# One inference step of a hybrid decoder: retention and memory attention of the prompt placed between the steps of the sample's latent attention

## The chip, the core and the metric

The kernel runs on one core of a Trainium2 chip, in float32. It is written for the engines directly: each engine has its own list of instructions, which it works off in order, and semaphores are waited for and counted up. TensorE (PE) multiplies matrices and writes to PSUM, VectorE (DVE) and ScalarE (ACT) do elementwise work, GpSimd (POOL) does elementwise work in SBUF and issues the gathers, and SyncE (SP) issues the other DMAs. The metric is the device time of one execution in microseconds.

## What is computed

One layer for a prompt of 2048 tokens and for a sample of 8 sequences with one new token each and 16384 tokens in a paged cache. The two parts that matter here are these, cut from the reference:

```python
def retention(q, k, v, state0):            # prompt: 16 chunks of 128 tokens, 4 heads of 128
    def step(S, inp):
        qb, kb, vb = inp
        sc = jnp.einsum('bihd,bjhd->bhij', qb, kb) * intra[None]
        o = (jnp.einsum('bhij,bjhe->bihe', sc, vb)
             + jnp.einsum('bihd,bhde->bihe', qb * q_dec[None, :, :, None], S))
        S = S * s_dec[None, :, None, None] + jnp.einsum('bjhd,bjhe->bhde', kb * k_dec[None, :, :, None], vb)
        return S, o
def mem_attend(q, mk, mv):                 # prompt: 256 memory tokens
    s = jnp.einsum('bthd,bmhd->bhtm', q, mk).astype(jnp.float32) * MEM_SCALE
    p = jax.nn.softmax(s, axis=-1).astype(mv.dtype)
    return jnp.einsum('bhtm,bmhd->bthd', p, mv).reshape(B, T, MEM_W)
def mla_sample(q_lat, q_pe, ckv_new, kpe_new, pool_ckv, pool_kpe, page_table):
    ckv_past = pool_ckv[page_table].reshape(DB, -1, KV_LORA)      # 8 x 16384 x 256
    kpe_past = pool_kpe[page_table].reshape(DB, -1, MLA_ROPE)     # 8 x 16384 x 64
    s_past = jnp.einsum('bqhc,bkc->bhqk', q_lat, ckv_past) + jnp.einsum('bqhr,bkr->bhqk', q_pe, kpe_past)
...
```

The output of retention is normalised per head (`head_norm`) and multiplied with a gain; it is joined with the others in `merge`.

## The kernel before

The kernel is a row of stages. Each stage is a function that allocates its own SBUF, PSUM and semaphores, and ends with a barrier of all engines: keys and values of the memory, the input projection, the sample's preparation, `sample_attention`, `prompt_retention_memory`, `prompt_latent_attention`, `merge`. The next stage loads its constants after the barrier.

**sample_attention** (names `sa_`) works through the cache in 64 steps of 2048 tokens. GpSimd gathers the latents (`nat`, 16 KB a partition, L1577) and the rope part (`kp`, 4 KB a partition, L1579) of step g into buffer g % DEEP, with DEEP = 4; from step 4 on it first waits until the values of step g-4 are done. In step g, VectorE turns the two halves of `nat` and then `kp` (L1612, the functions `turn(g, 0..2)`). After the first of them comes the row maximum of step g-1 (`new_low`, L1618, L1619), after the second the accumulation of step g-2 (`add_up`, L1627, L1630). TensorE multiplies the first turned piece with the queries (`scores(g, 0)`, L1709), turns the probabilities of g-1 (`pull_probs`, L1722), does `scores(g, 1)`, then the values of g-1 (`values`, L1733), which read `nat` and free its buffer, then `scores(g, 2)`. ScalarE does the exponential and one copy (L1672, L1673, L1681). PSUM holds two banks each of scores, turned probabilities and outputs.

**prompt_retention_memory** (names `rm_`) works through 16 blocks of 128 tokens, in loops of two. GpSimd rotates queries and keys (`rotate`: four products L620, L622, their sum `qk` L631, the decayed keys `kd` L636). TensorE turns queries and keys (L786, L790), multiplies queries with memory keys (L796), makes the state's increment (L804), the masked scores (L810), the outputs (L818, L819), turns the probabilities (L826), multiplies with memory values (L768) and turns the normalised output (L776). VectorE decays the queries (L660), takes the memory maximum (L664, L665), masks the scores (L668), inverts and applies the sum (L671, L673), updates the state (L679) and does the head's statistics, root, normalisation and gain (L683 to L700). Seven banks or pairs of banks of PSUM are used.

## Time and profile before

| | us |
|---|---|
| Median of three runs | 2814.61 |
| The three runs | 2814.0 to 2818.64 |
| The profiled execution's own time | 2821.66 |
| Its span | 2820.0 |
| Stage of the sample's latent attention, from its first DMA to that of the next stage | 1080.62 to 1582.75 |
| Stage of retention and memory attention, likewise | 1582.75 to 1838.61 |
| TensorE / VectorE / ScalarE / GpSimd busy in the span | 2339.9 / 1295.5 / 534.5 / 286.3 |

Times in the profile are counted from the span's start. A share of busy time over the whole span is a mean over stages with quite different limits, so the stages are to be read one by one.

### The profile page before, as it was taken

What the parts mean: (1) busy time and instruction counts of PE and PEld (TensorE: products, weight loads), DVE (VectorE), ACT (ScalarE), POOL (GpSimd) and SP (SyncE); (2) the same over time, 40 slices, a digit from 0 to 9 for tenths busy, and PEclk for the clock granted to TensorE, in tenths of its full rate; (3) what the DMA queues carried; (4) which work ended last, traced back from release to release, by engine and by line L of the source; (5) the groups of instructions that cost most, each with busy time, mean ns of one, the idle gap of its engine ahead of it and who ended that gap; (6) DMA issues with size and microseconds to landing.
All of it is one profiled execution on the core that took longest, in us unless ns stands there. A gap on an engine that the chain in (4) does not pass through costs nothing. (4 is left out here: it accounts for less than half of the span.)

```text
span 2820.0 us, 49617 instructions
## 1 busy us (share of the span) xinstructions
PE 2339.9 (83%) x20723; PEld 1925.0 (68%) x20723; DVE 1295.5 (46%) x2890; ACT 534.5 (19%) x1094; POOL 286.3 (10%) x244
## 2 busy tenths in 40 slices
PE   4499999999999685777777577748889999969998
PEld 2399999978888464555555366636766777757886
DVE  1711111110101243999888388836555444335554
ACT  1410010010100000111111133313333333332110
POOL 0000000000000001222222266500000000000000
PEclk8599999999999756999999799969999999989999
DMA  4221121111211515999999233221100000045542
GB/s 174 100 82 66 57 72 64 56 69 60 75 45 45 200 42 197 379 368 372 371 351 369 83 121 121 88 87 37 31 19 25 19 19 7 5 145 166 174 149 69
DMA packets 128029, 351.00 MB, mean 124 GB/s; under 512 B 13400, under 2 KB 74832, under 8 KB 117624
## 3 DMA queue, kind: packets, MB, share of 16 engines
q1 hardware_dynamic: 105088, 163.37, 17.0%
q0 software_dynamic: 22784, 185.35, 17.0%
q8 instruction: 121, 1.98, 0.3%
q14 instruction: 36, 0.29, 0.0%
HBM read 285.22 MB, written 63.46 MB: 124 GB/s over the span
## 5 line engine op out<-in xcount | busy, mean ns | idle before, releaser
L454 DVE COPY pj_stage<-pj_ps 128x280 f32<-128x280 f32 (+1 forms) x96 | 50.9, 530 | 642.0 <-PE pj_ps L473 334.8
L473 PE MATMUL pj_ps<-pj_wh,pj_xh 128*128 128x280 f32 x1024 | 299.1, 292 | 6.4 <-DVE pj_wl L447 6.4
L1612 DVE STREAM_TRANSPOSE sa_turned<-sa_nat 128x2048 f32<-128x2048 f32 x128 | 293.2, 2291 | 19.9 <-DMA sa_kp<-cache_kpe,sa_index 19.8
L473 PE MATMUL pj_ps<-pj_wl,pj_xh 128*128 128x280 f32 x1024 | 298.8, 292 | 0.0
L473 PE MATMUL pj_ps<-pj_wh,pj_xl 128*128 128x280 f32 x1024 | 298.8, 292 | 0.0
L1709 PE MATMUL sa_ps_s<-sa_turned,sa_q 128*32 128x128 f32 x5120 | 200.6, 288 | 100.8 <-DVE sa_turned L1612 69.8
L1709 PEld LDWEIGHTS sa_ps_s<-sa_turned,sa_q 128*32 128x32 f32 x5120 | 154.8, 115 | 134.4 <-DVE sa_turned L1612 76.0
L476 PE MATMUL pj_ps<-pj_xh,pj_wl 128*128 128x512 f32 x512 | 202.6, 396 | 0.0
L476 PE MATMUL pj_ps<-pj_xl,pj_wh 128*128 128x512 f32 x512 | 201.9, 394 | 0.0
L476 PE MATMUL pj_ps<-pj_xh,pj_wh 128*128 128x512 f32 x512 | 201.6, 394 | 0.0
L1031 DVE CUSTOM_DVE_ANT_0 la_row<-la_ps_s,la_causal 128x512 f32<-128x512 f32 (+3 forms) x160 | 97.6, 611 | 226.0 <-PE la_ps_s L1172 224.3
L473 PEld LDWEIGHTS pj_ps<-pj_wh,pj_xh 128*128 128x128 f32 x1024 | 193.4, 189 | 6.7 <-issue 6.5
L473 PEld LDWEIGHTS pj_ps<-pj_wl,pj_xh 128*128 128x128 f32 x1024 | 193.5, 189 | 0.0
L473 PEld LDWEIGHTS pj_ps<-pj_wh,pj_xl 128*128 128x128 f32 x1024 | 193.0, 188 | 0.0
L1196 PE MATMUL la_ps_o<-la_probsT,la_value 128*128 128x128 f32 x1088 | 145.6, 281 | 48.9 <-ACT la_probsT L1105 48.9
L1196 PEld LDWEIGHTS la_ps_o<-la_probsT,la_value 128*128 128x128 f32 x1088 | 132.6, 193 | 60.6 <-ACT la_probsT L1105 37.6
L436 ACT COPY pj_stage<-pj_ps 128x280 f32<-128x280 f32 (+1 forms) x96 | 44.0, 458 | 623.1 <-PE pj_ps L473 333.7
L1461 PE MATMUL mg_ps<-mg_wh,mg_ch 128*128 128x512 f32 (+1 forms) x408 | 129.0, 398 | 20.6 <-DVE mg_wl L1391 16.8
L1733 PE MATMUL sa_ps_o<-sa_nat,sa_p_turned 128*16 128x256 f32 x2048 | 133.0, 389 | 6.0 <-issue 5.5
L1461 PE MATMUL mg_ps<-mg_wl,mg_ch 128*128 128x512 f32 (+1 forms) x408 | 127.7, 395 | 0.0
L1461 PE MATMUL mg_ps<-mg_wh,mg_cl 128*128 128x512 f32 (+1 forms) x408 | 127.5, 394 | 0.0
L1577 POOL DMA_INDIRECT sa_nat<-cache_ckv,sa_index x64 | 60.0, 937 | 641.5 <-DVE sa_index L1601 332.4
(337 smaller groups left out, 4106.1 us busy)
## 6 DMA issues: line engine op xcount, KB each, us to landing
s_zn<-pj_stage SPq DMA_DIRECT2D x32, 560.0 KB, 3.0
s_zt<-pj_stage SPq DMA_DIRECT2D x16, 1024.0 KB, 3.8
rm_z<-s_zn SPq DMA_DIRECT2D x16, 768.0 KB, 4.3
mg_cat<-s_cat SPq DMA_DIRECT2D x16, 768.0 KB, 6.3
mg_gate<-s_zt SPq DMA_DIRECT2D x16, 768.0 KB, 8.0
pj_raw<-w_in POOLq DMA_DIRECT2D x8, 1120.0 KB, 6.7
pn_x<-x_prompt SPq DMA_DIRECT2D x4, 2048.0 KB, 9.1
pj_raw<-w_in POOLq DMA_DIRECT2D x8, 1024.0 KB, 5.9
```

Source lines behind the costliest of these rows:

```text
L436: act.copy(stage_view(u, w, natural), ps[:, u % QUAD, 0:(w if natural else 512)]).then_inc(ev_act, 1)
L454: dve.tensor_copy(stage_view(u, w, natural), ps[:, u % QUAD, 0:(w if natural else 512)])\
L473: mm = pe.matmul(ps[:, u % QUAD, 0:w], x[:, k, u * P:(u + 1) * P], wt[:, j, k, 0:w], **flags)
L476: mm = pe.matmul(ps[:, u % QUAD, :], wt[:, j, k, m * P:(m + 1) * P], x[:, k, c * 512:(c + 1) * 512], **flags)
L1031: dve.tensor_tensor_reduce(out=row[:, s, c * P:(c + w) * P], in0=ps_s[:, (first_chunk[u] + n) % 3, 0:w * P], in1=m, scale=1.0, scalar=-3.0 ...
L1196: mm = pe.matmul(ps_o[:, h, :], value[:, c + x, h * HD:(h + 1) * HD], probsT[:, g % 3, x, :], start=(c + x == 0), stop=(c + x == b))
L1461: mm = pe.matmul(ps[0:w, j, n * 512:(n + 1) * 512], a[:, c, :], wt[:, c, n * 512:(n + 1) * 512], start=(c == 0 and a is hi and wt is wh), ...
L1577: pool.indirect_dma_start(out=nat[:, g % DEEP, :, :].rearrange("p t c -> p (t c)"), out_offset=None, in_=ckv_rows, in_offset=where).then_i ...
L1612: dve.transpose(turned[:, s, a:z, :, :].rearrange("p c x q -> p x c q"), of.rearrange("p x (c q) -> p x c q", q=QR)).then_inc(t_ok, 1)
L1709: mm = pe.matmul(ps_s[j * QR:(j + 1) * QR, s, 0:TQ * QR], q32[:, u, c, :], turned[:, s, c, j * TQ:(j + 1) * TQ, :].rearrange("p x q -> p ( ...
L1733: mm = pe.matmul(ps_o[j * QR:j * QR + ROWS_Q, s, 0:KVL], p_turned[:, s, x, j, :], nat[:, g % DEEP, TQ * j + x, :], start=(x == 0), stop=(x ...
```

## The change

The two stages become one, `sample_attention_and_retention`. The work of block b is cut into parts that stand at fixed places of the steps 4b to 4b+4, written out without loops; the helper `begun(g, k)` gives the block whose k-th step g is. So that all fits, buffers are cut: DEEP is 3 in place of 4, `ps_p` and `ps_o` of latent attention have one bank each in place of two, and retention works with three shared PSUM areas (`bank_a`, `bank_b`, `bank_m`) and single `qk`, `kd`, `cat_r`, `cat_m`. The scaling of the memory probabilities, the normalisation of retention's output and its gain go from VectorE to ScalarE; the gain is applied to the turned output. The constants of both parts are loaded at the start, and VectorE, ScalarE, TensorE and GpSimd wait for those of retention before their first step.

```diff
-DEEP = 4
+DEEP = 3
+STRIDE = STEPS // BLOCKS
-        ps_p = r.ps("ps_p", [P, 2, 512])
-        ps_o = r.ps("ps_o", [P, 2, 512])
+        ps_p = r.ps("ps_p", [P, 512])
+        ps_o = r.ps("ps_o", [P, 512])
+        def begun(g, after):
+
+            b, rest = divmod(g - after, STRIDE)
+            return b if rest == 0 and 0 <= b < BLOCKS else None
...
+                pool.wait_ge(m_consts, 16 * M_CONSTS)
                 pool.wait_ge(index_ok, 1)
                 for g in range(STEPS):
                     if g >= DEEP:
...
+                    if begun(g, 1) is not None:
+                        rotate(begun(g, 1))
...
                     if 1 <= g <= STEPS:
                         new_low(g - 1)
+                    if begun(g, 1) is not None:
+                        decay_queries(begun(g, 1))
+                    if begun(g, 2) is not None:
+                        mask_scores(begun(g, 2))
+                        invert_total(begun(g, 2))
+                    if begun(g, 3) is not None:
+                        new_state(begun(g, 3))
+                        head_statistics(begun(g, 3))
                     if g < STEPS:
                         turn(g, 1)
                     if g >= 2:
                         add_up(g - 2)
+                    if begun(g, 1) is not None:
+                        memory_top(begun(g, 1))
...
+                def turn_queries_keys(b):
+                    pe.wait_ge(rotated, b + 1)
+                    if b >= 1:
+                        pe.wait_ge(cat_m_ok, b)
+                        pe.wait_ge(cat_r_ok, b)
...
-                for g in range(STEPS + 1):
+                pe.wait_ge(m_consts, 16 * M_CONSTS)
+                for g in range(STEPS + 2):
                     if g < STEPS:
                         scores(g, 0)
-                    if g >= 1:
+                    if 1 <= g <= STEPS:
                         pull_probs(g - 1)
                     if g < STEPS:
                         scores(g, 1)
-                    if g >= 1:
+                    if begun(g, 0) is not None:
+                        turn_queries_keys(begun(g, 0))
+                    if begun(g, 1) is not None:
+                        add_to_state(begun(g, 1))
+                    if begun(g, 2) is not None:
+                        retention_values(begun(g, 2))
+                    if begun(g, 3) is not None:
+                        turn_memory(begun(g, 3), 1)
+                    if 1 <= g <= STEPS:
                         values(g - 1)
                     if g < STEPS:
                         scores(g, 2)
+                    if begun(g, 0) is not None:
+                        memory_scores(begun(g, 0))
+                    if begun(g, 1) is not None:
+                        retention_scores(begun(g, 1))
+                    if begun(g, 2) is not None:
+                        turn_memory(begun(g, 2), 0)
+                    if begun(g, 3) is not None:
+                        memory_values(begun(g, 3))
+                        turn_retention(begun(g, 3))
```

On GpSimd, the gathers of the changed kernel are L1362 and L1364. Before, there are only pairs of gathers in a row. Now the rotation of block b follows the gather of step 4b+1:

```order
L1362 DMA sa_nat<-cache_ckv,sa_index 128x4096
L1364 DMA sa_kp<-cache_kpe,sa_index 128x1024
L1337 TENSOR_TENSOR rm_prod_cos<-rm_z,rm_rot 128x8x64
L1339 TENSOR_TENSOR rm_prod_sin<-rm_z,rm_rot 128x8x64
L1337 TENSOR_TENSOR rm_prod_cos<-rm_z,rm_rot 128x8x64
L1339 TENSOR_TENSOR rm_prod_sin<-rm_z,rm_rot 128x8x64
L1346 TENSOR_TENSOR rm_qk<-rm_prod_cos,rm_prod_sin 128x1024
L1352 TENSOR_TENSOR rm_kd<-rm_qk,rm_k_decay 128x512
```

Six operations have come between the gather of step 4b+1 and that of 4b+2.

On TensorE, a step of latent attention in the middle of its stage, from `scores(g, 0)` to `scores(g, 2)`, before:

```order
L1709 MATMUL sa_ps_s<-sa_turned,sa_q 32x128 x16
L1722 MATMUL sa_ps_p<-sa_pull,sa_probs 32x64 x16
L1709 MATMUL sa_ps_s<-sa_turned,sa_q 32x128 x16
L1733 MATMUL sa_ps_o<-sa_nat,sa_p_turned 16x256 x16
L1709 MATMUL sa_ps_s<-sa_turned,sa_q 32x128 x8
```

and now, for a step g = 4b:

```order
L1622 MATMUL sa_ps_s<-sa_turned,sa_q 32x128 x16
L1635 MATMUL sa_ps_p<-sa_pull,sa_probs 32x64 x16
L1622 MATMUL sa_ps_s<-sa_turned,sa_q 32x128 x16
L1656 MATMUL rm_bank_a<-sa_ident,rm_qk 128x128 x4
L1659 MATMUL rm_bank_b<-sa_ident,rm_qk 128x128 x4
L1646 MATMUL sa_ps_o<-sa_nat,sa_p_turned 16x256 x16
L1622 MATMUL sa_ps_s<-sa_turned,sa_q 32x128 x8
L1668 MATMUL rm_bank_m<-rm_mkT,rm_mq 128x256 x4
```

The transposes of the rotated queries and keys stand in front of the values of step g-1, the memory scores behind the step's last scores.

On VectorE, a step of latent attention before:

```order
L1612 STREAM_TRANSPOSE sa_turned<-sa_nat 128x16x4x32
L1618 TENSOR_REDUCE sa_step_top<-sa_ps_s 128x1
L1619 SCALAR_TENSOR_TENSOR sa_low<-sa_step_top,sa_low 128x1
L1612 STREAM_TRANSPOSE sa_turned<-sa_nat 128x16x4x32
L1627 SCALAR_TENSOR_TENSOR sa_acc<-sa_acc,sa_ratio,sa_total 128x1
L1630 SCALAR_TENSOR_TENSOR sa_acc<-sa_acc,sa_ratio,sa_ps_o 128x256
L1612 STREAM_TRANSPOSE sa_turned<-sa_kp 128x16x2x32
```

and now, for a step g = 4b+3 (the row of "..." leaves out the root's eleven small operations):

```order
L1399 STREAM_TRANSPOSE sa_turned<-sa_nat 128x16x4x32
L1405 TENSOR_REDUCE sa_step_top<-sa_ps_s 128x1
L1406 SCALAR_TENSOR_TENSOR sa_low<-sa_step_top,sa_low 128x1
L1447 SCALAR_TENSOR_TENSOR rm_state<-rm_state,rm_bank_b 128x128 x4
L1452 BN_STATS rm_stats<-rm_bank_m 128x6 x4
L1455 BN_AGGR rm_mean_var<-rm_stats 128x2 x4
L1457 TENSOR_SCALAR rm_var<-rm_mean_var 128x4
...
L1461 SCALAR_TENSOR_TENSOR rm_shift<-rm_mean_var,rm_root 128x4
L1399 STREAM_TRANSPOSE sa_turned<-sa_nat 128x16x4x32
L1414 SCALAR_TENSOR_TENSOR sa_acc<-sa_acc,sa_ratio,sa_total 128x1
L1417 SCALAR_TENSOR_TENSOR sa_acc<-sa_acc,sa_ratio,sa_ps_o 128x256
```

State, statistics and root of block b stand between the first and the second transpose of that step.

## Rows read from the trace of the kernel before

**Rows 1.** Busy time by stage, latent attention of the sample, then retention and memory.

```profile
core 0: us, PE busy (x) PEld busy (x) DVE busy (x) ACT busy (x) POOL busy (x), PEclk, DMA share, GB/s
1080.62:1582.75 502.13, 348.92 (x9243) 260.59 (x9243) 421.37 (x471) 65.11 (x257) 119.96 (x128) 0.92 0.86 339
1582.75:1838.61 255.86, 173.13 (x1216) 156.28 (x1216) 191.56 (x561) 72.77 (x192) 151.70 (x96) 0.91 0.35 115
```

**Rows 2.** Timeline, one clean step: start, duration, engine, line, operation, count, idle before.

```profile
1154.25 2.27 DVE L1612 STREAM_TRANSPOSE sa_turned<-sa_nat 128x2048 f32<-128x2048 f32 x1
...
1156.45 0.25 DVE L1618 TENSOR_REDUCE sa_step_top<-sa_ps_s 128x1 f32<-128x128 f32 x1
...
1156.81 2.30 DVE L1612 STREAM_TRANSPOSE sa_turned<-sa_nat 128x2048 f32<-128x2048 f32 x1
...
1159.17 1.08 PE L1709 MATMUL sa_ps_s<-sa_turned,sa_q 128*32 128x128 f32 x32 [0.81 <-DVE sa_turned L1612]
...
1160.06 1.91 PE L1733 MATMUL sa_ps_o<-sa_nat,sa_p_turned 128*16 128x256 f32 x32
1160.68 2.27 DVE L1612 STREAM_TRANSPOSE sa_turned<-sa_nat 128x2048 f32<-128x2048 f32 x1
...
1161.79 0.62 PE L1709 MATMUL sa_ps_s<-sa_turned,sa_q 128*32 128x128 f32 x16
1162.28 0.94 POOL L1577 DMA_INDIRECT sa_nat<-cache_ckv,sa_index  x1 [4.26 <-PE sa_ps_o L1733]
...
1163.52 0.94 POOL L1579 DMA_INDIRECT sa_kp<-cache_kpe,sa_index  x1 [0.30 <-issue]
```

**Rows 3.** Rope gather's landing, its transposes, start of the stage, TensorE's waits.

```profile
DMA to landing us min/median/max: 9.3/10.5/16.5
...
L1612 DVE STREAM_TRANSPOSE sa_turned<-sa_kp x64: 1201/1236/1241, 1109.5 to 1560.7; 128x1024 f32<-128x1024 f32 x64
...
1095.21 1.01 POOL L1577 DMA_INDIRECT sa_nat<-cache_ckv,sa_index  x1 [332.37 <-DVE sa_index L1601]
...
1105.06 4.50 DVE L1612 STREAM_TRANSPOSE sa_turned<-sa_nat 128x2048 f32<-128x2048 f32 x2 [10.13 <-DMA sa_kp<-cache_kpe,sa_index]
...
PE sa_ps_s L1709 <- issue: 30.9, 22, 3.2
```

**Rows 4.** Timeline of a late block of retention, VectorE and TensorE.

```profile
1820.79 1.22 DVE L664 TENSOR_REDUCE rm_top<-rm_ps_m 128x4 f32<-128x1024 f32 x1
...
1822.12 0.69 DVE L668 TENSOR_TENSOR rm_scT<-rm_ps_sc,rm_mask 128x512 f32<-128x512 f32 x1
...
1822.87 0.49 PE L818 MATMUL rm_ps_a<-rm_z,rm_scT 128*128 128x128 f32 x2 [0.35 <-DVE rm_scT L668]
...
1824.20 0.18 DVE L671 RECIPROCAL rm_inv<-rm_total 128x4 f32<-128x4 f32 x1 [1.39 <-ACT rm_probs L720]
...
1824.53 0.39 PE L819 MATMUL rm_ps_a<-rm_state,rm_qT 128*128 128x128 f32 x2
...
1825.56 0.88 DVE L679 SCALAR_TENSOR_TENSOR rm_state<-rm_state,rm_ps_st 128x128 f32<-128x128 f32 x4
1825.70 1.09 PE L826 MATMUL rm_ps_m<-rm_ident,rm_probs_n 128*128 128x128 f32 x8 [0.78 <-DVE rm_probs_n L673]
...
1830.18 1.37 DVE L695 TENSOR_SCALAR rm_normed<-rm_ps_a,rm_mean_var,rm_root 128x128 f32<-128x128 f32 x4
```

**Rows 5.** Timeline of the first rotation on GpSimd: first product and sum.

```profile
1595.08 1.25 POOL L620 TENSOR_TENSOR rm_prod_cos<-rm_z,rm_rot 128x512 f32<-128x512 f32 x1 [50.98 <-DMA rm_mq<-s_zt]
...
1600.28 2.34 POOL L631 TENSOR_TENSOR rm_qk<-rm_prod_cos,rm_prod_sin 128x1024 f32<-128x1024 f32 x1 [0.16 <-POOL rm_prod_sin L622]
```

**Rows 6.** A constant's landing (us last), a small operation's mean, the stage's last accumulation.

```profile
rm_gain<-ret_gn_g SPq DMA_DIRECT2D x1, 256.0 KB, 5.9
...
L665 DVE TENSOR_SCALAR rm_bias<-rm_top 128x4 f32<-128x4 f32 x16 | 12.5, 780 | 0.6
...
1569.63 0.48 DVE L1630 SCALAR_TENSOR_TENSOR sa_acc<-sa_acc,sa_ratio,sa_ps_o 128x256 f32<-128x256 f32 x1 [4.51 <-PE sa_ps_o L1733]
```

More of the change, by code:

```diff
@@ new lines, in invert_total, with new_state @@
+                def invert_total(b):
+                    dve.wait_ge(exp_ok_m, b + 1)
+                    if b >= 1:
+                        dve.wait_ge(pn_ok, b)
+                    dve.reciprocal(m_inv[:, :], m_total[:, :]).then_inc(inv_ok, 1)
+                def new_state(b):
+                    dve.wait_ge(out_ps, b + 1)
+                    dve.wait_ge(st_ps, b + 1)
+                    for h in range(HEADS):
+                        last = dve.scalar_tensor_tensor(state[:, h, :], state[:, h, :], S_DEC[h], bank_b[:, h, :], ALU.mult, ALU.add)
+                    last.then_inc(state_ok, 1)
@@ new lines, in head_statistics @@
+                def head_statistics(b):
+                    for h in range(HEADS):
+                        last = dve.bn_stats(stats[:, h, :], bank_c[:, h, :])
+                    link(last)
+                    for h in range(HEADS):
+                        last = dve.bn_aggr(mean_var[:, h, :], stats[:, h, :])
+                    link(last)
+                    link(dve.tensor_scalar(var[:, :], mean_var[:, :, 1], EPS, None, ALU.add))
+                    if b >= 1:
+                        dve.wait_ge(normed_ok, b)
+                    inverse_root(dve, link, var[:, :], root[:, :], tmp[:, :])
+                    dve.scalar_tensor_tensor(shift[:, :], mean_var[:, :, 0], -1.0, root[:, :], ALU.mult, ALU.mult)\
+                       .then_inc(root_ok, 1)
@@ new lines, in memory_out, with normalise @@
+                def memory_out(b):
+                    act.wait_ge(pv_ps_m, b + 1)
+                    if b >= 1:
+                        act.wait_ge(cat_m_out, 16 * b)
+                    act.copy(cat_m[:, :, :], bank_a[:, :, :]).then_inc(cat_m_ok, 1)
+                def normalise(b):
+                    act.wait_ge(root_ok, b + 1)
+                    if b >= 1:
+                        act.wait_ge(rT_ps, b)
+                    for h in range(HEADS):
+                        last = act.activation(normed[:, h, :], bank_c[:, h, :], ACT.Identity, bias=shift[:, h:h + 1],
+                                              scale=root[:, h:h + 1])
+                    last.then_inc(normed_ok, 1)
@@ new lines, in turn_memory @@
+                def turn_memory(b, n):
+                    pe.wait_ge(pn_ok, b + 1)
+                    if n == 1:
+                        pe.wait_ge(pT_ok, 2 * b + 1)
+                    halves = bank_m[:, 2:4, :].rearrange("p h (m q) -> p h m q", m=2)
+                    for h in range(2):
+                        for x in range(2):
+                            mm = pe.transpose(halves[:, h, x, :], m_probs[:, 2 * n + h, x * P:(x + 1) * P], ident[:, :])
+                    mm.then_inc(pT_ps, 1)
@@ new lines, in memory_values, with turn_retention @@
+                def memory_values(b):
+                    pe.wait_ge(pT_ok, 2 * b + 2)
+                    for h in range(HEADS):
+                        for n in range(2):
+                            mm = pe.matmul(bank_a[:, h, :], mv[:, n, h * HD:(h + 1) * HD], probsT[:, h, n, :],
+                                           start=(n == 0), stop=(n == 1))
+                    mm.then_inc(pv_ps_m, 1)
+                def turn_retention(b):
+                    pe.wait_ge(normed_ok, b + 1)
+                    pe.wait_ge(state_ok, b + 1)
+                    for h in range(HEADS):
+                        mm = pe.transpose(bank_b[:, h, :], normed[:, h, :], ident[:, :])
+                    mm.then_inc(rT_ps, 1)
@@ L1738, in _ @@
+                pe.wait_ge(m_consts, 16 * M_CONSTS)
+                for g in range(STEPS + 2):
                     if g < STEPS:
                         scores(g, 0)
-                    if g >= 1:
+                    if 1 <= g <= STEPS:
                         pull_probs(g - 1)
```

539 lines of the change are left out of this document (227 added, 312 removed).

## The prediction

> **What bounds the kernel now.** I read the busy table by stage first [rows 1]. The sample's latent attention takes 502.1 us and retention with memory attention 255.9 us; the change touches these 758 us and nothing else. In the first VectorE is busy 421 of 502 us and the DMA engines 0.86 of the time, in the second TensorE 173 and VectorE 192 of 256 us, with DMA at 0.35. So the first stage has little room on two resources, and the second has latencies to hide.
>
> Then the timeline of one clean step [rows 2]. Times in a step are counted from the start S of its first transpose. The three transposes, the row maximum and the two accumulations fill VectorE: the next step begins 6.43 us later (1154.25 to 1160.68). On the average a step takes 7.16 us, since the 64 transposes of keys' rope part start between 1109.5 and 1560.7 [rows 3]: 0.7 us a step goes to disturbances, among them fetches of instructions on TensorE (30.9 us before the score matmuls alone [rows 3]). TensorE ends the values of the step before at S + 7.72 (1161.97), and GpSimd issues the next gather at once, at 1162.28. It was waiting: with four buffers the gather g waits for the values of g-4. The rope half follows 1.24 us later (1163.52).
>
> How long does a gather need? The rope half lands at least 9.3 us after its own issue [rows 3], so both halves have landed at least 10.54 us after the first issue; with an empty queue at the start of the stage it was 9.85 us (1095.21 to 1105.06 [rows 3]). I take 10.54, the steady value. With four buffers a gather has two steps of 6.43 us and the rest of the third to arrive, 19.3 - 8.0 = 11.3 us: just enough.
>
> **The change: three buffers.** The gather g+2 is now issued after the values of g-1, which end in step g. It must be there two steps after S. So two steps cost at least 7.72 + 0.31 + 10.54 = 18.6 us, 9.3 us a step instead of 6.43, before anything is added. That is the heart of my forecast: the stage passes from a bound of work to a loop of latencies, and what is put between a step's start and the end of its values lengthens that loop.
>
> **The change: what is added between.** Four kinds of step follow each other; A is the one before a multiple of four, then B, C, D. On VectorE, ahead of the second transpose: in C 0.69 us (decayed queries, the same form as the mask), in D 0.69 + 0.18 (mask, reciprocal), in A the state, the statistics and the root, 4.62 us from 1825.56 to 1830.18 and one small operation of 0.2, 4.82 in all. After it, in C, the memory maximum, 1.22 and a small operation like the reciprocal, 0.2 [rows 4]. Together 7.8 us a block; the scaled probabilities, the normalisation and the gain go to ScalarE. On TensorE, ahead of the values: in B eight transposes, 1.09 us; in C four matmuls, half of the eight's 2.05 us (1822.87 to 1824.92), so 1.03; in D these eight, 2.05; in A four transposes, 0.55 [rows 4]. ScalarE's parts (at most 4 x 0.5 us in a step) lie beside TensorE's and VectorE's work; they cost nothing while that cover of 2 us is there. Loads and stores of retention, 1.66 MB a block, find a queue that idles more than a third of the time. On SP they are queued in the order of the blocks, more than a block ahead of need, so nothing.
>
> On GpSimd the rotation stands behind every fourth gather: four products and the sum take 7.54 us (1595.08 to 1602.62 [rows 5]), then the decayed keys. TensorE meets the wait for the rotation in B, in front of the values of A.
>
> **The loop, one block (four steps).** From the end of the values in A: 0.31 to GpSimd, 2.5 for the two issues, 7.54 of rotation, 1.09 of transposes, 1.91 of values [rows 2]: 13.35. Gather of D: 0.31 + 10.54 = 10.85. Step D to the end of the values in it: 2.56 to the end of the maximum and the new minimum, 0.87, 2.36 for the second transpose, 0.89 of scores, 2.05, 1.91: 10.64. Then TensorE ends the scores 0.44 later (1162.41), and A, whose first transpose is over by then, goes on: maximum and minimum 0.36 (1156.45 to 1156.81), 4.82, 2.36, 0.89, 0.55, 1.91: 11.33. Sum **46.2 us**. A second loop, gathers of C and A without the rotation, is 10.85 + (2.56 + 0.69 + 2.36 + 0.89 + 1.03 + 1.91 = 9.44) + 10.85 + (2.56 + 4.82 + 2.36 + 0.89 + 0.55 + 1.91 = 13.09) = 44.2. The first is the longer. To it comes a part of the disturbances. Before they cost 4 x 0.73 = 2.9 us in four steps; the queue is now less full and half of them fall beside waits, so between 0 and 3, and I take 1.0: 47.2 us a block.
>
> **Start and end.** GpSimd now waits for seven more constants ahead of its first gather; like-sized ones land 5.9 us after issue [rows 6], so the first gather starts about 6 us late, at 1101.3, and step 0 at 1111.2. Step 3 ends its values at 6.5 + 9.44 + 10.85 + 13.09 = 39.9 us after that, 1151.1. Fifteen blocks of 47.2 us lead to 1859. The last memory values, copies and value matmuls take some 8.4 us (VectorE waited 4.51 us for the last values before 1569.63 [rows 6], and some 4 us of retention stand ahead of them now), and from there the old end of the stage, 1569.63 to 1582.75, is 13.1. The next stage begins at about 1881 instead of 1838.6 [rows 1]: **+42 us**. One stage's start (10 to 15 us) is saved in this already. The profiled execution has a span of 2820.0 and 2821.66 us in all, 7 above the median of 2814.61; I add the difference to the median: **2857 us**.
>
> **A rule against the trace.** The Trainium skill, Trainium Kernel Development and Optimization, Best Practices, says that double-buffering gets DMA beside compute; by it three buffers are more than enough and the first rival below holds. The trace has GpSimd waiting for the values at four [rows 2], which speaks against it. The skill's DMA: Bandwidth & Descriptors (Anatomy of one DMA, SWDGE) gives 2.0 us plus bytes over 436 GB/s, an estimate of 8.0 us for the 2.62 MB of a step where the trace has 10.54; by it the loops are 43.7 and 39.1 us and the time is about 2820.
>
> **Rivals.** (1) The ring is not what binds; the busiest engine is. Then VectorE's 4 x 7.16 + 7.8 = 36.4 us is a block (TensorE's 348.92 / 64 x 4 + 173.13 / 16 is 33), and the time 2857 - 15 x 10.8 = 2695, **faster** by 4%. For it: the idle time of the second stage disappears and all engines have room. Against: the 11.3 us that a gather has now. It decides where 10.54 us of landing would be hidden; any loop under 44.4 us a block (47.2 - 42/15) makes the change a gain, so a landing of 7.7 us would do. 12%, and 8% for something between it and 2800. (2) The rotation is not on the path (GpSimd starts it earlier, or TensorE's wait is covered): 44.2 + 1.0 = 45.2, and 2857 - 30 = 2827. 18%, with 2800 to 2835. (3) It is worse: the new loads and stores share the DMA engines with a gather that now counts in full (landing at the median 10.5 + 1.24 = 11.7), VectorE and GpSimd disturb each other, as where an operation on 128x4 numbers took 780 ns on the mean beside the rotation [rows 6], disturbances stay at 2.9. That is 1.2 + 0.9 + 1.9 = 4 us more a block, 2917. 15%. (4) That the change does not do what it says is excluded by the order of the instructions.
>
> **Chances and range.** The forecast, 2835 to 2885: 47%. A difference under 0.2%, 5.6 us, can hardly be told from none. Slower by more than that: the forecast, rival 3 and two thirds of rival 2, some more: 68%. Within it 8%. Faster: rival 1, the case between and the rest of rival 2: 24%. The range, with rival 1 left out below and the far end of rival 3 above: 2795 to 2915.
>
> **What would show it.** In the changed profile: steps of 11 to 12 us instead of 7.2; VectorE's first transpose waiting for the rope gather in most steps, some 20 us in the whole stage before and well over 100 after; VectorE's and DMA's busy share in the stage down to 0.7 and 0.6; GpSimd's gather released by the values each time; TensorE's transposes of the rotated queries waiting some 5 us for GpSimd in each block; the stage about 800 us long. A first transpose that seldom waits for DMA makes me wrong in the direction of rival 1. A landing time much under 10 us does too. No wait of TensorE for the rotation is rival 2.

## The result, and the profile after

| | before | after |
|---|---|---|
| Median, us | 2816.62 (4 runs, 2814.0 to 2822.51) | 2929.24 (4 runs, 2928.31 to 2935.09) |
| Span of the profiled execution | 2820.0 | 2928.5 |
| The two stages, then the one | 758.0 | 859.9 |
| Mean time from one block's rotation to the next | | 51.2 |

The changed kernel takes 1.0401 times as long, with an interval of 1.0379 to 1.0424: slower by 113 us, where +42 was forecast and +100 was the end of the range. The stage takes 101.9 us more than the two did together, the stages behind it 6.6.

The row of the whole stage, and of 500 us in its middle, answers to [rows 1]. Columns: stretch, its length, busy time of PE, PEld, DVE, ACT, POOL with their instructions, TensorE's granted clock, DMA share, GB/s.

```profile
1080.62:1940.55 859.93, 596.05 (x10459) 437.04 (x10459) 595.19 (x949) 193.48 (x641) 254.43 (x224) 0.82 0.63 232
...
1200.00:1700.00 500.00, 362.26 (x6390) 266.12 (x6380) 362.76 (x550) 119.30 (x395) 157.08 (x138) 0.83 0.65 238
```

TensorE does the same 10459 matmuls as in the two stages before and is busy 596 us with them instead of 522: they became slower, not more. The granted clock fell with it: 0.82 over the whole stage, where the two stages before had 0.92 and 0.91 [rows 1]. VectorE's and DMA's shares, 0.73 and 0.65 in the middle, are about those that the prediction asked for.

Who waited for whom in the changed kernel: us in all, times, longest.

```profile
POOL sa_nat L1362 <- PE sa_ps_o L1646: 518.7, 61, 13.2
...
PE sa_ps_s L1622 <- DVE sa_turned L1399: 161.6, 57, 20.4
DVE sa_turned L1399 <- DMA sa_kp<-cache_kpe,sa_index: 159.2, 58, 17.6
...
PE rm_bank_a L1656 <- POOL rm_qk L1346: 71.5, 15, 4.8
DVE sa_step_top L1405 <- PE sa_ps_s L1622: 68.8, 40, 4.0
```

This is the loop that was forecast: each gather released by the values, VectorE waiting for the gather, TensorE waiting 4.8 us a block for the rotation.

The rotations' sums and the rope transposes, each with the start of its first and its last:

```profile
L1346 POOL TENSOR_TENSOR rm_qk<-rm_prod_cos,rm_prod_sin x16: 2339/2343/2347, 1108.8 to 1876.6; 128x1024 f32<-128x1024 f32 x16
```

```profile
L1399 DVE STREAM_TRANSPOSE sa_turned<-sa_kp x64: 1202/1237/1243, 1115.5 to 1915.9; 128x1024 f32<-128x1024 f32 x64
```

Fifteen blocks in 767.8 us are 51.2 us each, where 47.2 were forecast; 63 steps in 800.4 are 12.7.

One block of the changed kernel on the timeline. Columns: start, duration, engine, line, operation, count, idle before and what ended it. A to D are the steps as in the prediction, and V_A is the value matmuls (L1646) in step A, and so on: V_A starts at 1303.20, V_B at 1317.66, V_D at 1342.87, the next V_A at 1355.57. GpSimd issues the next gather 0.3 us after they end.

```profile
1300.29 1.93 PE L1622 MATMUL sa_ps_s<-sa_turned,sa_q 128*32 128x128 f32 x32 [4.12 <-DVE sa_turned L1399]
...
1303.20 2.60 PE L1646 MATMUL sa_ps_o<-sa_nat,sa_p_turned 128*16 128x256 f32 x32
...
1306.12 0.94 POOL L1362 DMA_INDIRECT sa_nat<-cache_ckv,sa_index  x1 [11.21 <-PE sa_ps_o L1646]
...
1308.32 1.30 POOL L1337 TENSOR_TENSOR rm_prod_cos<-rm_z,rm_rot 128x512 f32<-128x512 f32 x1
...
1308.95 4.35 DVE L1414 SCALAR_TENSOR_TENSOR sa_acc<-sa_acc,sa_ratio,sa_total 128x1 f32<-128x1 f32 x1
...
1313.36 2.34 POOL L1346 TENSOR_TENSOR rm_qk<-rm_prod_cos,rm_prod_sin 128x1024 f32<-128x1024 f32 x1
...
1315.76 1.11 PE L1656 MATMUL rm_bank_a<-sa_ident,rm_qk 128*128 128x128 f32 x4 [4.77 <-POOL rm_qk L1346]
...
1317.66 3.62 PE L1646 MATMUL sa_ps_o<-sa_nat,sa_p_turned 128*16 128x256 f32 x32
...
1321.58 0.97 POOL L1362 DMA_INDIRECT sa_nat<-cache_ckv,sa_index  x1 [4.75 <-PE sa_ps_o L1646]
...
1332.26 2.31 DVE L1399 STREAM_TRANSPOSE sa_turned<-sa_nat 128x2048 f32<-128x2048 f32 x1 [3.82 <-DMA sa_kp<-cache_kpe,sa_index]
...
1334.62 1.28 PE L1622 MATMUL sa_ps_s<-sa_turned,sa_q 128*32 128x128 f32 x32 [3.56 <-DVE sa_turned L1399]
...
1337.87 1.93 PE L1622 MATMUL sa_ps_s<-sa_turned,sa_q 128*32 128x128 f32 x32 [1.05 <-DVE sa_turned L1399]
...
1342.87 1.92 PE L1646 MATMUL sa_ps_o<-sa_nat,sa_p_turned 128*16 128x256 f32 x32
```

The two large terms that are not TensorE's are as forecast: D's gather lands 10.68 us after its issue (10.54 forecast), the rotation takes 7.38 (7.54). But the 32 value matmuls, which take 1.92 us in V_D at a granted clock of 1.00 (2.4 GHz), take 3.62 after the wait for the rotation, at a granted clock of 0.50 (1.2 GHz), and 2.60 in V_A, at 0.72; 32 score matmuls take 1.93 instead of 1.08, at 0.50 too.

One row stands out on VectorE: the accumulation of the sum (L1414), an operation on 128x1 numbers that takes 0.18 us elsewhere, takes 4.35 beside GpSimd's products. Here it costs nothing: VectorE then still waits 2.26 us for the next gather, and TensorE waits for the rotation until 1315.76. The experiments come back to it.

### The profile page after: what moved, and what is told of

Same layout as the page of the kernel before. It is cut to its first block and busy times, and to the rows that moved or that the text cites. A ratio compares the mean times of both kernels' runs of the same rounds, so it can differ in the third digit from the quotient of the medians.

```text
span 2928.5 us, 49100 instructions
## 1 busy us (share of the span) xinstructions
PE 2418.7 (83%) x20723; PEld 1950.2 (67%) x20723; DVE 1279.2 (44%) x2809; ACT 590.6 (20%) x1286; POOL 269.0 (9%) x244
## 5 line engine op out<-in xcount | busy, mean ns | idle before, releaser
L1622 PE MATMUL sa_ps_s<-sa_turned,sa_q 128*32 128x128 f32 x5120 | 209.3, 308 | 162.4 <-DVE sa_turned L1399 161.6
L1646 PE MATMUL sa_ps_o<-sa_nat,sa_p_turned 128*16 128x256 f32 x2048 | 155.0, 454 | 1.0 <-ACT sa_p_turned L1524 1.0
L1362 POOL DMA_INDIRECT sa_nat<-cache_ckv,sa_index x64 | 60.7, 948 | 856.6 <-PE sa_ps_o L1646 518.7
```

The lines of the kernel that those rows point to most:

```text
L1362: pool.indirect_dma_start(out=nat[:, g % DEEP, :, :].rearrange("p t c -> p (t c)"), out_offset=None, in_=ckv_rows, in_offset=where).then_i ...
L1622: mm = pe.matmul(ps_s[j * QR:(j + 1) * QR, s, 0:TQ * QR], q32[:, u, c, :], turned[:, s, c, j * TQ:(j + 1) * TQ, :].rearrange("p x q -> p ( ...
L1646: mm = pe.matmul(ps_o[j * QR:j * QR + ROWS_Q, 0:KVL], p_turned[:, s, x, j, :], nat[:, g % DEEP, TQ * j + x, :], start=(x == 0), stop=(x == ...
```

## Experiments on the loop: ring and rotation

**Three buffers alone.** The kernel before, with DEEP = 3 and nothing else.

```diff
-DEEP = 4
+DEEP = 3
```

> The kernel before with one line changed, three gather buffers in place of four; the two stages stay apart. If the ring of buffers is what binds (my forecast), two steps cost 7.72 + 0.31 + 10.54 = 18.6 us, 9.3 us a step in place of 7.16, and the whole becomes 64 x 2.14 = 137 us longer, about 2952 us, with VectorE waiting for the rope gather in nearly every step. If TensorE's clock also falls in those waits, it is more, up to 2990. If the ring does not bind and the cost of the change is the placing of retention between the steps, this stays within 20 us of the kernel before.

Measured 2984.6 us, ratio 1.059 [1.057, 1.061]. VectorE's waits for the rope gather and TensorE's for VectorE:

```profile
PE sa_ps_s L1709 <- DVE sa_turned L1612: 221.4, 45, 12.6
DVE sa_turned L1612 <- DMA sa_kp<-cache_kpe,sa_index: 198.3, 37, 9.9
```

The ring of three is a loop of latencies, as argued: 167 us on 64 steps, 2.6 us a step where the sum gave 2.1. The expectation had left room for this, up to 2990 us if the clock falls, and the granted clock is 0.80 between 1200 and 1700 us: the same symptom without anything of the retention.

**Four buffers in the changed kernel.** They fit into SBUF.

```diff
-DEEP = 3
+DEEP = 4
```

> The changed kernel with one line changed back, four gather buffers. If the ring binds in the changed kernel, a block falls from 51.3 us to what the busiest engine asks, VectorE with 36.4 us plus up to 4 us in which it is held beside the rotation, so 37 to 42 us, and the time from 2929 to between 2730 and 2790, under the kernel before. If the placing of retention is the cause, the time stays within 20 us of 2929.

Measured 2860.6 us, ratio 1.015 [1.012, 1.018]: 69 us faster than the changed kernel, but far from what was expected. VectorE waits only 18.9 us for gathers now, so the ring is gone; the block is 45.9 us. What took its place is told in the section on the hold.

**The rotation's four products left out** (constants stand in their place, so the prompt's retention isn't computed), once with three buffers and once with four.

```diff
-                    for a in range(2):
-                        pool.tensor_tensor(prod_cos[...], zz[...], cos[...], ALU.mult).then_inc(g_chain, 1)
-                        pool.tensor_tensor(prod_sin[...], zz[...], sin[...], ALU.mult).then_inc(g_chain, 1)
-                    pool.wait_ge(g_chain, 4 * (b + 1))
+                    if b == 0:
+                        pool.memset(prod_cos[...], 0.5).then_inc(g_chain, 1)
+                        pool.memset(prod_sin[...], 0.25).then_inc(g_chain, 1)
+                        pool.wait_ge(g_chain, 2)
```

> The changed kernel with its three buffers; the rotation's four products on GpSimd are left out (constants stand in their place, so the prompt retention computes something else), its sum and the decayed keys stay. Theory A (the rotation is on the loop, from the values to the next values, and TensorE's clock falls because of its waits): 5.0 us of products leave the loop of 52.4 us, TensorE's wait of 4.8 us for the rotated queries disappears, and the block is 45 to 47.5 us: 2825 to 2860 us. If the clock recovers with that wait, a block is up to 3 us less again, 2780 to 2825 us. Rival B (rotation beside the path, the gathers' loop alone sets the block): 2910 to 2930 us.

> Four buffers and the rotation's four products left out (constants in their place, so the prompt retention computes something else). Theory A: against four buffers alone the 7.1 us a block of held operations disappear, 46.4 to about 39 us: 2740 to 2760 us; the floor is VectorE's work, 36.4 us a block, 2710. Rival B (the clock of TensorE, 2.4 GHz only part of the time, and the order of its groups set the block at four buffers): 2830 to 2860 us.

Measured 2898.0 (ratio 1.0285 [1.0255, 1.0315]) and 2785.9 us (0.9894 [0.9865, 0.9923]). With three buffers 5.0 us of work a block went and TensorE's wait for the rotation with it, yet only 31 us came back, 2.1 a block. That is the distance between the two loops of the prediction (46.2 and 44.2): the second takes over at once, and it too is slower than forecast, 49.1 us against 45.2. Its gather of C lands 11.86 us after its issue on the mean, 1.3 more than the 10.54 of the sum; the granted clock is 0.85. Both expectations missed this result; the working of the prediction had it. With four buffers the same edit gives 75 us, again between the two expectations.

## Experiments on the order of TensorE's work

**Values ahead of the inserted groups**, three buffers.

```diff
+                    if 1 <= g <= STEPS:
+                        values(g - 1)
                     if begun(g, 0) is not None:
                         turn_queries_keys(begun(g, 0))
...
-                    if 1 <= g <= STEPS:
-                        values(g - 1)
```

> The changed kernel with three buffers; on TensorE the inserted part of each step stands behind the values of the step before, no longer in front of them, so that the gather is released earlier. If the ring binds, the loop loses the wait for the rotation's transposes (the gather then follows the rotation directly), 2 us of values of retention in step D and 0.5 to 1 in A: 51.3 becomes 44 to 47 us a block and the time 2820 to 2865. If TensorE's own order does not matter, 2929.

Measured 2890.0 us, ratio 1.0266 [1.0243, 1.0288]: 39 us of the 65 to 110 expected. A row of VectorE shows what ate into it (count, busy time, mean of one in ns, idle before):

```profile
L1406 DVE SCALAR_TENSOR_TENSOR sa_low<-sa_step_top,sa_low 128x1 f32<-128x1 f32 x64 | 90.2, 1410 | 2.2
```

The new minimum (L1406), 160 ns in the changed kernel, takes 5.5 us in each of 15 blocks: with the values earlier it meets GpSimd's products, 5.0 us too much a block. The section on the hold tests this in other kernels; in this one it wasn't taken away.

**TensorE kept busy.** 24 added transposes, which nothing reads, ahead of the wait for the rotated queries, 24 ahead of the second scores in A, 16 at the end of C (line of the first shown).

```diff
+                        for _ in range(24):
+                            pe.transpose(bank_a[:, 0, :], ident[:, :], ident[:, :])
                     pe.wait_ge(rotated, b + 1)
```

> The changed kernel with added transposes of the unit matrix, which nobody reads, where TensorE waits: 24 ahead of the wait for the rotation, 16 at the end of step C, 24 ahead of the second score matmuls of step A. If the 4 to 5 us a block by which my sum was too small are TensorE's lower granted clock (0.84 in place of 0.95), the clock rises over 0.92 and the time falls by 40 to 70 us, to 2860 to 2890. If the clock is not the cause, the added work is in the way and the time is 2929 or more.

Measured 2925.2 us, ratio 1.037 [1.034, 1.04]. The clock rose from 0.83 to 0.93 and the time hardly moved. It looked like the end of the theory of the clock, but the profile has a wait of TensorE that the changed kernel doesn't have:

```profile
PE sa_ps_p L1635 <- ACT sa_probs L1516: 61.4, 14, 4.4
```

In these 14 blocks the minimum (L1406) takes 4.3 to 5.5 us. What that means shows only in a kernel further down. Two kernels with fewer transposes at other places came first: 16 ahead of the first scores in C and 20 ahead of the second in A, without and with the products.

> merged_without_products (2898.0 us, 49.1 us a block from one rotated block to the next, granted clock 0.83 to 0.86), with 36 small transposes a block added on TensorE that nothing reads: 16 ahead of the first scores of the step after a block's first, 20 ahead of the second scores of the step with the head statistics. There TensorE stood for 4.25 and 4.98 us, and 24 such transposes took 4.9 us at 1.2 GHz, so they end before what it waits for. Theory A (the time above the forecast is TensorE at 1.2 GHz after its waits): what follows these waits runs at 2.4 GHz, some 4 us of the loop come back, a block of 45 to 46 us, 2840 to 2860 us. Rival B (the clock falls, but the work at 1.2 GHz lies beside the gathers): 2890 to 2905 us.

> The changed kernel with its rotation and three buffers (2929.2 us, 51.2 us a block), with the same 36 added transposes at the same two places, and none ahead of the wait for the rotated queries, where those of merged_kept_busy stood in the way. Theory A: the scores, inserted groups and values after the two waits run at 2.4 GHz, 2 to 3 us a block less, 2885 to 2900 us; what follows the wait for the rotation stays slow. Rival B: 2922 to 2935 us.

Measured 2864.5 (ratio 1.0171) and 2917.9 us (1.0355 [1.0318, 1.0391]). Without the products 34 us came back, more than rival B allows and less than A wants; with them 11, again between the two. Then all three waits of the longer loop, 30, 14 and 30 transposes, made to fit them:

> The changed kernel, with 74 added small transposes a block on TensorE that nothing reads, placed into the waits of the longer loop and made to fit them: 30 (3.6 us at 2.4 GHz) ahead of the wait for the rotated queries (4.77 us), 14 ahead of the first scores of the step with the mask (3.6 us), 30 ahead of the second scores of the step with the statistics (4.1 us). In merged_kept_busy_two_waits the block was 50.5 us, and what followed the wait for the rotation still ran at 1.2 GHz: transposes 2.0 and values 3.6 us instead of 1.1 and 1.9. Theory A (what is above the forecast is TensorE at 1.2 GHz): these run at 2.4 GHz, 2.5 us come off, and the rest of the two other steps: 47.2 to 48.5 us a block, 2865 to 2895 us, which is the forecast's block. Rival B (the second loop, or something not in the forecast, sets the block): 2905 to 2925 us.

Measured 2926.2 us, ratio 1.0409 [1.0372, 1.0446], clock 0.92: nothing gained. But its timeline tells why. A block's end there:

```profile
1292.54 0.94 POOL L1362 DMA_INDIRECT sa_nat<-cache_ckv,sa_index  x1 [9.21 <-PE sa_ps_o L1646]
...
1294.74 1.28 POOL L1337 TENSOR_TENSOR rm_prod_cos<-rm_z,rm_rot 128x512 f32<-128x512 f32 x1
1294.82 4.86 DVE L1406 SCALAR_TENSOR_TENSOR sa_low<-sa_step_top,sa_low 128x1 f32<-128x1 f32 x1
...
1300.49 1.08 PE L1635 MATMUL sa_ps_p<-sa_pull,sa_probs 128*32 128x64 f32 x32 [4.39 <-ACT sa_probs L1516]
```

The steps D and A had shrunk to 10.53 us (gather landed to the end of V_D; forecast 10.64) and 11.39 (V_D to V_A; forecast 11.33). With that the gather of B, issued after V_D at 1281.15, lands at 1292.30, just when V_A ends; its first transpose, 2.31 us, goes ahead of VectorE's minimum (L1406), and the minimum, 0.16 us of work on 128x1 numbers, now starts 0.08 us behind GpSimd's first product. It ends 4.86 us later, when the four products are done. The same happens in 13 of the 15 blocks. From here on this is called the hold: a small VectorE operation stands still beside GpSimd's work. Exponential, turned probabilities and V_B come late, and TensorE has a new wait of 4.39 us, after which it is slow again (1.08 us for 32 matmuls that take 0.65).

## Experiments on the hold

**Products behind the minimum.** The last kernel, with GpSimd waiting for the minimum first; and the same edit alone in the changed kernel.

```diff
                     if begun(g, 1) is not None:
+                        if g >= STRIDE:
+                            pool.wait_ge(low_ok, g - 1)
                         rotate(begun(g, 1))
```

> merged_kept_busy_three_waits (2926.2 us, 51.3 us a block), and GpSimd also waits for VectorE's minimum of the step before it begins a block's products. In that run three of the four steps took what was forecast (10.5 and 11.4 us for the last two), but the minimum, an operation on 128x1 numbers with both inputs in SBUF, came 0.1 us behind the start of the products and stood 4.9 us beside them instead of 0.16; TensorE waited 4.4 us for the probabilities and fell to 1.2 GHz again. Theory A (clock and hold together are the excess over the forecast): both are gone, 47 to 48.5 us a block, 2865 to 2895 us. Rival B (something else keeps the block at 51): 2915 to 2930 us.

> The changed kernel, and GpSimd waits for VectorE's minimum of the step before it begins a block's products; nothing is added on TensorE. In the changed kernel the minimum is 160 ns on the mean, before the products as it is. Theory A (there the hold is not what lengthens the loop, the clock is): no change, 2922 to 2936 us. Rival B (the hold costs here too): under 2910 us.

Measured 2854.3 us (ratio 1.0131 [1.0098, 1.0164]) and 2930.1 us (1.04 [1.0383, 1.0418]). The first is the forecast's 2857, and 11 us under its own expectation. Its stretch in the middle and one pass from V_D's gather to V_B's:

```profile
1200.00:1700.00 500.00, 429.18 (x7854) 341.81 (x7846) 366.20 (x631) 128.03 (x431) 171.87 (x152) 0.99 0.72 268
```

```profile
1276.27 0.94 POOL L1362 DMA_INDIRECT sa_nat<-cache_ckv,sa_index  x1 [10.18 <-PE sa_ps_o L1648]
...
1287.66 0.93 POOL L1362 DMA_INDIRECT sa_nat<-cache_ckv,sa_index  x1 [9.21 <-PE sa_ps_o L1648]
...
1289.87 0.16 DVE L1408 SCALAR_TENSOR_TENSOR sa_low<-sa_step_top,sa_low 128x1 f32<-128x1 f32 x1
...
1290.11 1.29 POOL L1337 TENSOR_TENSOR rm_prod_cos<-rm_z,rm_rot 128x512 f32<-128x512 f32 x1 [0.26 <-DVE sa_low L1408]
...
1291.35 1.27 POOL L1339 TENSOR_TENSOR rm_prod_sin<-rm_z,rm_rot 128x512 f32<-128x512 f32 x1
...
1292.17 0.47 DVE L1416 SCALAR_TENSOR_TENSOR sa_acc<-sa_acc,sa_ratio,sa_total 128x1 f32<-128x1 f32 x1
...
1298.60 1.92 PE L1648 MATMUL sa_ps_o<-sa_nat,sa_p_turned 128*16 128x256 f32 x32
...
1300.83 0.96 POOL L1362 DMA_INDIRECT sa_nat<-cache_ckv,sa_index  x1 [2.18 <-PE sa_ps_o L1648]
```

The clock is 0.99, and from one gather to the next V_D to V_A takes 11.39 us (forecast 11.33) and V_A to V_B 13.17 (forecast 13.35). The mean block is 46.4 us; the loop's sum was 46.2. In the changed kernel itself the wait changes nothing: there the minimum comes before the products anyway. So the four kernels with neither cure, with the transposes alone, with the wait for the minimum alone and with both take 2929.2, 2926.2, 2930.1 and 2854.3 us. It is the clock that lengthens the changed kernel's loop; the hold stands behind it and takes over as soon as the clock is cured alone. One thing moved along: the hold of the sum's accumulation (L1416 here) is shorter too, 525 ns on the mean instead of 1196. That this is worth nothing was tested only with four buffers, below.

**The hold with four buffers.** In merged_deep4 the products run one step earlier, beside the head statistics. VectorE and GpSimd there:

```profile
1327.66 1.28 POOL L1337 TENSOR_TENSOR rm_prod_cos<-rm_z,rm_rot 128x512 f32<-128x512 f32 x1
...
1328.21 4.41 DVE L1457 TENSOR_SCALAR rm_var<-rm_mean_var 128x4 f32<-128x4 f32 x1
...
1332.66 2.36 POOL L1346 TENSOR_TENSOR rm_qk<-rm_prod_cos,rm_prod_sin 128x1024 f32<-128x1024 f32 x1
1332.85 2.19 DVE L103 TENSOR_SCALAR rm_root<-rm_tmp 128x4 int32<-128x4 int32 x1
```

Moved one gather earlier, with the sum's 128x1 accumulation on VectorE as before and moved to ScalarE:

```diff
-                    if begun(g, 1) is not None:
-                        rotate(begun(g, 1))
+                    if begun(g, 0) is not None:
+                        rotate(begun(g, 0))
```

```diff
-                    dve.scalar_tensor_tensor(acc[:, u, KVL:KVL + 1], acc[:, u, KVL:KVL + 1], ratio[:, s:s + 1], total[:, s:s + 1],
-                                             ALU.mult, ALU.add)
...
+                    act.activation(acc[:, u, KVL:KVL + 1], acc[:, u, KVL:KVL + 1], ACT.Identity, bias=total[:, s:s + 1],
+                                   scale=ratio[:, s:s + 1]).then_inc(sum_ok, 1)
```

> The changed kernel with four gather buffers, and the rotation one gather earlier in GpSimd's order, so it runs in the step before the one with the head statistics. With four buffers alone the time was 2860.6 and a block 46.4 us; in it the 128x4 operations of the head statistics stood still for 7.1 us a block beside GpSimd's products. Theory A (VectorE's small operations are held by GpSimd's products): the hold leaves the statistics, and only the 128x1 accumulation of the step's sum meets the products now, held for up to 4.4 us: a block of 42 to 44 us, 2795 to 2825 us. Rival B (the 7 us are the operations' own cost there, or the loop over the score matmuls sets the block): no change, 2850 to 2865 us.

> The same as four_buffers_rotation_earlier, and the 128x1 accumulation of the sum, whose two inputs are both in SBUF, is done by ScalarE, so that it is not among VectorE's operations beside the products. Theory A: no hold is left on VectorE but the minimum of the next step, a block of 39 to 40 us, 2745 to 2775 us, faster than the kernel before. Rival B: as its partner without the moved sum, within 6 us.

Measured 2780.8 us (ratio 0.9871 [0.9843, 0.99]) and 2770.8 us (0.9833 [0.9804, 0.9862]): 80 us less than merged_deep4 with the first step alone, and both 1.3 to 1.7% faster than the kernel before. The first is faster than theory A's range. The move of the sum can't be told from nothing (the intervals overlap, the blocks are 40.1 and 40.3 us), though it took away 2.2 us of hold a block (L1414, 720 ns on the mean): in the stage VectorE waits 52.1 us for scores with the hold and 88.0 without it, so the hold had stood in the place of a wait.

Then TensorE's inserted groups behind the last scores of a step, or between values and last scores, with the rotation early:

```diff
-                    (inserted groups)
                     if 1 <= g <= STEPS:
                         values(g - 1)
                     if g < STEPS:
                         scores(g, 2)
+                    (inserted groups)
```

> four_buffers_rotation_earlier (2780.8 us, 40.1 us a block) with the inserted groups of TensorE behind the values and behind the last scores of a step, so that they are not ahead of the scores for which VectorE's maximum waits (62.6 us in all there). Theory A (VectorE is the bound now, at 0.86 busy, and its waits for the scores are what is left): 2 to 3 us a block less, 2735 to 2755 us. Rival B (the inserted work only moves from one side of the values to the other): 2772 to 2785 us.

> four_buffers_rotation_earlier with the inserted groups behind the values and ahead of the last scores. The values, and with them the next gather, are earlier by 1 us a step on the mean, the scores are not. Theory A (VectorE's waits for scores count, not the gather's start): 2772 to 2785 us, no change. Rival B (the gathers still set the time): 2735 to 2760 us.

Measured 2819.8 (ratio 1.0013) and 2859.0 us (1.0144): 39 and 78 us slower than with the order left alone, against both theories. The minimum (L1406) in the first and in the second, mean of one in ns after its busy time, 160 being its own:

```profile
L1406 DVE SCALAR_TENSOR_TENSOR sa_low<-sa_step_top,sa_low 128x1 f32<-128x1 f32 x64 | 55.4, 866 | 2.2
```

```profile
L1406 DVE SCALAR_TENSOR_TENSOR sa_low<-sa_step_top,sa_low 128x1 f32<-128x1 f32 x64 | 84.3, 1318 | 2.2
```

Earlier values mean an earlier rotation, and it meets the minimum. The last pair takes the holds away (wait for the minimum, sum on ScalarE), with the groups last and with the order left alone:

> four_buffers_earlier_groups_last (2819.8 us, 43.0 us a block; the minimum 866 and the sum's accumulation 446 ns on the mean where 160 and 179 are their own, 62 us too much in all) with both holds taken away: the products wait for the minimum, the 128x1 accumulation of the sum is on ScalarE. Theory A (the hold is why this order was slower than its partner): 39 to 40 us a block, 2755 to 2775 us. Rival B (the order itself costs): 2805 to 2825 us.

> four_buffers_rotation_earlier_sum_moved (2770.8 us, 40.3 us a block), and the products wait for the minimum, which stood at 255 ns on the mean instead of 160 there, 6 us in all. Theory A: at most these 6 us come back, 2762 to 2774 us. Rival B (the start of the rotation counts for more): 2776 us or more.

Measured 2773.4 us (ratio 0.9844 [0.9827, 0.986]) and 2770.7 us (0.9837 [0.982, 0.9854]), both theory A. The first gains 46 us over its partner with the holds (its rival B, that the order itself costs, would have left it at 2805 or more). All kernels with four buffers on one line, what stood still (busy time of VectorE's held operations over their own, in 16 blocks) beside the block:

| | held, us a block | block, us |
|---|---|---|
| rotation beside the statistics (merged_deep4) | 6.5 | 45.9 |
| the same, no products | 1.9 | 41.0 |
| rotation earlier | 2.2, on the sum | 40.1 |
| ... sum moved | 0.4 | 40.3 |
| ... groups last | 2.8 minimum, 1.1 sum | 43.0 |
| ... values first | 4.6 minimum, 0.5 sum | 45.3 |
| ... groups last, no hold | 0.1 | 40.1 |
| ... order left alone, no hold | 0.0 | 40.0 |

A hold of the statistics or of the minimum costs from half to somewhat more than its length (1.9 to 6.5 us held, 1.0 to 5.9 above the 40.0 of the last line); one of the sum's accumulation costs nothing.

## Why the prediction was wrong

**Right: what the change does.** Ring and rotation make a loop from values to values, and the kernel gets slower. DEEP = 3 alone costs 167 us. Landing, rotation, steps of 12.7 us (a little above the 11 to 12 asked for), the waits and the two shares are as listed under what would show it. Start and end are right too: the next stage starts at 1940.5 instead of the forecast 1881, 59.5 us later, and fifteen blocks of 51.2 instead of 47.2 us are 59.8. The rest of the miss, some 13 us, is the 6.6 us of the later stages and the 7 by which the profiled execution of before lay above its median, which I took off; that of after, 2930.17, lies 0.9 above its own.

**Wrong: the sum "The loop, one block".** Its terms of TensorE (values 1.91, scores 0.89, transposes 1.09 and 0.55, outputs 2.05) come from [rows 2, 4], where TensorE waits 0.81 us at most. In the loop it waits three times a block for 3.6 to 4.8 us (the three rows with such a wait above), and the granted clock falls to the lower level, 0.50, at or shortly behind each. In the block shown, from V_A's start to the next V_A's: V_A +0.69, V_B +1.71, the eight transposes +0.81 (1.90 from the first's start to the values'), the second scores in D +0.85, the outputs +1.08, the second scores in A +0.85, the memory transposes +0.50. That is 6.5 us; the block's excess is 52.4 - 46.2 = 6.2 (it is a longer one; the mean block, 51.2, is 5.0 above the sum). With the clock held up and the minimum kept clear of the products the block is 46.4 us and the time 2854.3 us: the terms themselves were right, their clock was not. The forecast knew the clock column [rows 1] and didn't use it.

**Wrong: disturbances, 1.0 us.** This was the place for it, and rival 3 had a wrong list: its 4 us were landing, VectorE beside GpSimd and the old disturbances. On the loop of the forecast none of them grew: D's gather lands after 10.69 us on the mean of 15, VectorE's hold in the changed kernel costs nothing, and TensorE's idle time that nothing in the profile ends, which the prediction took for fetches, is 9.8 us in the stage, where the score matmuls alone had 30.9. (The gather of C, which lies on the second loop only, lands after 11.78.) That rival 3 would have given 2917, near the 2929, is luck. The chances didn't add up either: the forecast, rival 3 and two thirds of rival 2 are 74%, not 68.

**Missed: the hold.** The 780 ns of [rows 6] were named, in rival 3, as a small general burden of 0.9 us. It is up to 4 or 5 us a block, and its cost depends on which operation meets the products: nothing in the changed kernel, where it is the sum's accumulation, and several us in merged_deep4 (the statistics), merged_kept_busy_three_waits and four_buffers_earlier_groups_last (the minimum), as the kernels show in which it was taken away. The minimum is held in merged_values_first, merged_kept_busy and four_buffers_earlier_values_first too, where its cost wasn't isolated. For the miss of the forecast itself it isn't needed.

**Rivals 1 and 2.** Four buffers and the rotation out of the way give 2771, a gain, but with VectorE at 0.80 to 0.86 and not at its bound of 36.4 us a block (2695). So rival 1 was right in direction once both were gone, but not in size. Rival 2, the rotation off the path, is merged_without_products: 31 us under the changed kernel where 30 was worked out.

**Open** is what fills the 40 us of the best kernels above VectorE's 36.4; their clock is 0.91 to 0.92, and VectorE still waits for scores (L1408 behind L1630, 92.3 us in the one without holds). Open, too, is what the second loop has above its sum beyond the late gather of C: without the products and with a clock of 0.93 the block is 47.4 us, not 44.2.

## What to carry to other kernels

When a change turns a stage bound by work into a loop with waits of several us, price TensorE's share of the loop at the lower clock, and look at the granted clock of a stage that already waits like that. Before cutting a ring of buffers, add the landing time and the time from landing until the buffer is free and divide by the buffers: that is the least time of a step. Here a step's values run in the next step, so a buffer is in use for a whole step and 7.7 us: with three buffers (0.3 + 10.5 + 9.3 + 7.7) / 3 = 9.3 us (9.8 measured, at a lower clock), with four less than the 6.43 of the work. One buffer was worth 167 us, more than the 120 that the merging could hide at most by rival 1. Work on GpSimd that reads and writes SBUF is to be placed by which VectorE operation it meets: a tiny one on the critical path can cost as much as a whole run of GpSimd's instructions. And when a cure moves nothing, look for a new wait before dropping the theory.

## What the runs showed of the hardware

- **The hold.** A VectorE operation of 160 to 180 ns on 128x1 or 128x4 numbers from SBUF to SBUF (the scalar_tensor_tensor with two inputs in SBUF, the tensor_scalar with one) that starts beside GpSimd's tensor_tensor ends together with one of these, mostly with the last of an unbroken row: 4.35, 4.41 and 4.86 us beside four products of 1.25 each, 2.19 beside the sum. It isn't always the last: with the products behind the minimum, the sum's accumulation ended with the second product in 9 of 15 blocks (0.47 us in the rows above) and with the fourth in 6; in the kernel before, L665 of [rows 6] ended with the first in 12 of 15 (0.73 us). In merged_values_first the minimum starts 0.5 us ahead of the first product, during the rope gather's issue, and is held all the same (5.5 us; starts on GpSimd are rough in the profile). What decides this stays open. Transposes of 128x2048 (2.30 us) and reductions from PSUM (0.25 to 0.29) aren't touched. The Trainium skill (GPSIMD Engine Reference, Key points) says that GpSimd shares its SBUF interfaces with VectorE and contends with VectorE's instructions that have two SBUF inputs or run in a 2-port mode; the traces agree for the operations with two such inputs, and show the tensor_scalar with one held too; whether that ran in a 2-port mode they don't show. The Trainium skill (SBUF — State Buffer, SBUF: two separate sides) says that whoever starts first has the shared ports for the whole instruction; here it was mostly the whole row of four, not the one of 1.25 us.
- **The clock.** With waits of 3.6 to 4.8 us in each block, the same 10459 matmuls cost 74 us more of busy time (a granted clock of 0.82 instead of 0.92 and 0.91). The 32 value matmuls take 1.92 us at 1.00 and 3.62 at 0.50. 74 small transposes a block, 135 us of TensorE's time in all, raised the granted clock to 0.99 and, with the minimum kept clear of the products, were worth 75 us; the same wait for the minimum without them was worth nothing.
- **The landing** of a paired gather, where VectorE waited for it (58 of 64), was 9.54 us at least and 10.85 at the median in the changed kernel, with a DMA share of 0.65 and retention's loads beside it. Before, at 0.86, it was at least 10.54 and 11.7 at the median [rows 1, 3]. So the emptier queue made it about 1 us shorter, but not for every gather: that of C landed after 11.78 us on the mean, the others after 10.6 to 10.7. Why C's is later no run shows.
